# Row scales applied where outputs are drained, a new opening order, and packed queries in a two-block transformer kernel

## The reference

```python
mem_n = rmsnorm(mem, mem_norm_g)                      # 256 memory tokens
hn = rmsnorm(x, attn_norm_g[0])
proj = hn @ w_in                                      # c_q 384 | c_kv 256 | k_r 32 | q_cross 256
q = (rmsnorm(c_q, q_norm_g) @ w_uq).reshape(b, s, 12, 96)
q = concat([q[..., :64], rope(q[..., 64:], positions)])
kv = (rmsnorm(c_kv, kv_norm_g) @ w_ukv).reshape(b, s, 12, 64 + 64)
k = concat([kv[..., :64], broadcast(rope(k_r, positions))])
o = causal_dense_attention(q, k, kv[..., 64:])
cross = memory_cross_attention(q_cross, mem_n, w_mem_kv[i])
x = x + concat([o, cross]) @ w_o[i];  x = x + squared_relu_mlp(rmsnorm(x), ...)
```

## Time and profile before

| | |
|---|---|
| three timed runs | 1968.14, 1969.76, 1969.70 us (median 1969.7) |
| profiled execution | 1970.45 us, span 1968.5 us |
| busy in the span: TensorE, VectorE, ScalarE, GpSimd | 98%, 46%, 39%, 48% |
| chain that ended last | TensorE 90%, VectorE 5%, issue 3%, ScalarE 2% |
| mean granted TensorE clock | 0.989 of 2.4 GHz |

### The profile page before, as it was taken

How to read it: one execution, slowest core, us unless ns; L and a number is a source line. 1 busy time by engine, 2 the same in 40 slices (tenths; PEclk the granted TensorE clock), 3 DMA queues, 4 the chain that set the end, 5 groups by cost and what they waited for, 6 DMA issues and landing times.

```text
span 1968.5 us, 27142 instructions
## 1 busy us (share of the span) xinstructions
PE 1932.1 (98%) x9314; PEld 1590.0 (81%) x9314; DVE 897.3 (46%) x1840; ACT 770.5 (39%) x1375; POOL 944.3 (48%) x1236
## 2 busy tenths in 40 slices
PE   7999999999999999999999999999999999999999
PEld 6867878888888888788888876678988888888887
DVE  7877732222226585422223474676722345444200
ACT  4537743223233476432232452326832342232221
POOL 5750155555546542555555564432045546555653
PEclk9999999999999999999999999979999999999999
DMA  5330023232222301232323232111023223233332
GB/s 216 100 110 1 12 97 97 96 97 96 96 96 91 101 29 33 91 98 95 101 93 99 93 117 77 53 54 44 1 84 98 95 78 107 96 96 98 105 107 75
DMA packets 47086, 168.46 MB, mean 86 GB/s; under 512 B 5328, under 2 KB 5648, under 8 KB 46736
## 3 DMA queue, kind: packets, MB, share of 16 engines
q1 hardware_dynamic: 45792, 164.54, 25.7%
q10 hardware_dynamic: 1200, 2.64, 0.5%
HBM read 164.28 MB, written 2.10 MB: 85 GB/s over the span
## 4 chain that ended last, share of the span: by engine, by line
PE 90%; DVE 5%; issue 3%; ACT 2%; POOL 0%; DVEq 0%; POOLq 0%; ACTq 0%
PE bank L559 26%; PE bank L560 26%; PE bank L561 26%; PE bank L664 4%; PE bank L637 3%; PE bank L650 2%; DVE XL L1271 1%; ACT PROB L948 1%; PE bank L821 1%; PE bank L731 0%; PE bank L604 0%; POOL WL L520 0%; DVE KT L1284 0%; PE bank L616 0%; PE bank L661 0%
## 5 line engine op out<-in xcount | busy, mean ns | idle before, releaser
L520 POOL TENSOR_TENSOR WL<-RAW,WH 128x256 fp32r<-128x256 f32 x1208 | 927.0, 799 | 980.3 <-ACT WH L884 980.1
L559 PE MATMUL bank<-XH,WH 128*128 128x512 f32 (+2 forms) x1472 | 586.3, 398 | 5.7 <-DVE XL L1271 4.4
L560 PE MATMUL bank<-XL,WH 128*128 128x512 f32 (+2 forms) x1472 | 576.2, 391 | 0.0
L561 PE MATMUL bank<-XH,WL 128*128 128x512 f32 (+2 forms) x1472 | 575.8, 391 | 0.0
L884 ACT ACTIVATE WH<-RAW 128x1024 fp32r<-128x1024 f32 x302 | 317.2, 1052 | 360.0 <-PE bank L561 359.4
L559 PEld LDWEIGHTS bank<-XH,WH 128*128 128x128 f32 (+2 forms) x1472 | 276.5, 188 | 79.5 <-issue 10.4
L560 PEld LDWEIGHTS bank<-XL,WH 128*128 128x128 f32 (+2 forms) x1472 | 276.6, 188 | 61.7 <-issue 4.1
L561 PEld LDWEIGHTS bank<-XH,WL 128*128 128x128 f32 (+2 forms) x1472 | 276.6, 188 | 60.3
L559 PE MATMUL bank<-HH,WH 128*128 128x512 f32 x512 | 199.2, 389 | 0.0
L561 PE MATMUL bank<-HH,WL 128*128 128x512 f32 x512 | 199.2, 389 | 0.0
L560 PE MATMUL bank<-HL,WH 128*128 128x512 f32 x512 | 199.2, 389 | 0.0
(11 more groups left out here) (346 smaller groups left out, 2611.5 us busy)
## 6 DMA issues: line engine op xcount, KB each, us to landing
RAW<-stream SPq DMA_DIRECT2D x302, 512.0 KB, 3.6
X<-x SPq DMA_DIRECT2D x4, 512.0 KB, 7.0
out<-X SPq DMA_DIRECT2D x8, 256.0 KB, 4.6
MEM<-mem SPq DMA_DIRECT2D x1, 1024.0 KB, 10.9
W<-cmp_w ACTq DMA_DIRECT2D x1, 1024.0 KB, 4.8
KT<-KR ACTq DMA_DIRECT2D x1, 768.0 KB, 6.2
CT<-consts SPq DMA_DIRECT2D x1, 656.0 KB, 12.6
POSB<-pos_rows ACTq DMA_DIRECT2D x2, 256.0 KB, 2.6
```

What stands on the lines that cost most here:

```text
L520: ins = pool.tensor_tensor(WL[:, slot, c], RAW[:, slot, c], WH[:, slot, c].bitcast(F32), ALU.subtract)
L559: pe.matmul(dst, lhs[0], rhs[0], start=start, stop=False)
L560: pe.matmul(dst, lhs[0], rhs[1], start=False, stop=False)
L561: return pe.matmul(dst, lhs[1], rhs[0], start=False, stop=stop)
```

## The change

Six things change, all before the first attention.

1. **Opening.** SyncE loads the first eight gain columns, x 0, x 1, weight tile 0 and the rest of x in five pieces; the early constants and other gains move from ScalarE's queue to SyncE's, behind weight tile 1. VectorE sets ACC to ones, ScalarE reads one column of it, and TensorE multiplies it three times in fp32 into bank 7. ScalarE rounds tile 0 after two x tiles instead of one.
2. **Three outputs by passes.** Outputs 0 to 2 of in0 first go through the WH passes, then the WL passes. The small products move: sums(in0) after output 1 as before but inside this scheme, scales(in0) after 3, sums(mem) after 4, scales(mem) after 5, sums(c_kv) after 6, scales(c_q) after mem output 5 instead of 6.
3. **mem.** Its operand is mem times gain, rounded straight from MEM, with its remainder made by one VectorE pass early; the row scale (RBM) and column scale (RMEM) are applied when outputs are drained.
4. **c_kv and c_q.** The c outputs are drained by ScalarE without a scale; the operand is C32 times gain in one VectorE pass; the inner norm's scale comes out of sums over the unscaled c (`of_normed`, with the x scale) and is applied at the drains of keys (RBC), values (RKV, by ScalarE) and queries (ACC).
5. **Queries.** The weight columns are regrouped: three outputs of 128 rows hold the rope parts of four heads each, six outputs hold the plain parts of two heads each. The three rope outputs are scaled, rotated and added on 128 rows, and ScalarE places 32 rows per head; the six plain outputs are drained like the keys.
6. **Attention's entry** waits for all but two drains, and for the other two at its second and third unit.

```diff
-    up += [(3 + h // 3, (h % 3 * KQ + k) * QK, QK, k, 14 + h) for h in range(NH) for k in range(KQ)]
-    p.stage("up0", 7, 26, up)
+    up += shift(by_output(NROPE + NH // 2, KQ), 3, FIRST_Q)      # NROPE = 3, FIRST_Q = 14
+    p.stage("up0", 7, FIRST_Q + NROPE + NH // 2, up)
...
@ sync
-            for j in range(RING):
-                sp.dma_start(X[:, 2 * j:2 * j + 2, :], x[:, 2 * j:2 * j + 2, :]).then_inc(x_in[j], 16)
-                if j == 0:
+            sp.dma_start(GV[:, 0:KD], gains[:, 0:KD]).then_inc(signal("first_gains_in"), 16)
+            for first, n in X_PIECES:          # ((0, 1), (1, 1), (2, 2), (4, 2), (6, 2))
+                sp.dma_start(X[:, first:first + n, :], x[:, first:first + n, :]).then_inc(x_in[first], 16)
+                if first == 1:
                     load(0, 0, stream[0])
             load(1, 1, stream[1])
+            sp.dma_start(CT[:, 0:CONST_LATE], consts[:, 0:CONST_LATE]).then_inc(consts_in, 16)
+            sp.dma_start(GV[:, KD:], gains[:, KD:]).then_inc(consts_in, 16)
             load(2, 2, stream[2])
...
@ tensor
+            def warm_up():
+                pe.wait_ge(signal("acc_set"), 1)
+                for _ in range(3):
+                    ins = pe.matmul(BANK[7][:], ACC[:, 0:P], ACC[:], start=True, stop=True)
+                ins.then_inc(signal("acc_read"), 1)
+
+            def first_outputs(n, after):
+                steps = [plan.steps["in0"][j * KD:(j + 1) * KD] for j in range(n)]
+                for j in range(n):
+                    pe.wait_ge(hi_done, j + 1)
+                    for a, part in ((XH, "in0_x_hi"), (XL, "in0_x_lo")):
+                        for t, c, width, k, o, _, _, _ in steps[j]:
+                            if j == 0:
+                                pe.wait_ge(signal(part), k + 1)
+                            pe.matmul(BANK[o % RING][:], WH[:, t % RING, c:c + width], a[:, k, :],
+                                      start=k == 0 and part == "in0_x_hi", stop=False)
+                for j in range(n):
+                    pe.wait_ge(lo_done, j + 1)
...                                                # the WL products of output j, then after[j]
+            first_outputs(3, {1: sums("in0")})
+            dense(lambda _: plan.steps["in0"][3 * KD:], 0, operand(XH, XL), o0=plan.out0["in0"],
+                  after={3: [scales("in0", diagonal=TMP[:, 0, :])], 4: [sums("mem", NMEM)], 5: [scales("mem", NMEM)],
+                         6: [sums("c_kv")]})
...
+                pe.wait_ge(drained, plan.out0["up0"] + FIRST_Q + r + 1)      # rotate_query(r), r < 3
+                pe.matmul(BANK[6 + r % 2][:], const("rot_mla", 0, P), TMP[:, r % 2, :], start=True, stop=True)
...
@ scalar, in order
+            for m in range(KD): ... x_hi("in0", "attn0", m); after m == 1: keep_ahead(in0, 0)
+            keep_ahead(in0, 1); squares of x, with keep_ahead(in0, 2) after the fourth; keep_ahead(in0)
+            for m in range(KD):
+                act.activation(MH_[:, m, :], MEM[:, m, :], ACT.Copy, scale=gain("mem", m)).then_inc(signal("mem_hi"), 1)
+            std("in0"); keep_ahead(in0 + 2); c_out(0..2); keep_ahead(in0 + 3); squares of mem
+            c_out(3); keep_ahead(in0 + 4); c_out(4); std("mem", NMEM); keep_ahead(in0 + 5)
+            c_square("c_kv", 0, 0); keep_ahead(in0 + 6); c_square("c_kv", 0, 1); std("c_kv")
+            keep_ahead(in0 + 7); keep_ahead(memo); act.wait_ge(products_done, plan.out_mark[in0 + 7])
+            for j in range(KKV + KQ):
+                act.activation(XH[:, j, :], C32[:, j, :], ACT.Copy, scale=norm_gain).then_inc(signal("c_hi"), 1)
...
+                for i in range(4):                 # for each rope output r
+                    ins = act.activation(QT0[HD:QK, 4 * r + i, :], TMP[ROPE * i:ROPE * (i + 1), r % 2, :], ACT.Copy)
+                ins.then_inc(signal("q0_placed"), 1)
...
@ vector, in order
+            remainders of x; acc_read; add_square("in0", 0..7); remainders of mem (one pass each)
             scale_columns("in0", D, diagonal=TMP[:, 0, :])
             for m in range(KD):
                 add_square("mem", m, NMEM)
             scale_rows("in0", RBC)
-            c_out(0..2); scale_columns("mem", D, NMEM)
             angles0(0)
-            c_out(3); scale_rows("mem", ACC, NMEM); mem in two passes a tile, c_out(4) inside
+            scale_columns("mem", D, NMEM, dst=RMEM)
             angles0(1)
+            scale_rows("mem", RBM, NMEM)
             add_square("c_kv", 0..1); KR; memory queries
+            for j in range(KKV + KQ):
+                dve.scalar_tensor_tensor(XL[:, j, :], C32[:, j, :], norm_gain, XH[:, j, :].bitcast(F32),
+                                         ALU.mult, ALU.subtract).then_inc(signal("c_lo"), 1)
...
+            for m in range(6):
+                both_halves(up0 + m, KT0[0:HD, :, :], m, RBC)
+            def query_rope(r):
+                if r >= 2:
+                    dve.wait_ge(signal("q0_placed"), r - 1)
+                dve.tensor_tensor(TMP[:, r % 2, :], output(up0 + FIRST_Q + r)[:], ACC[:], ALU.mult).then_inc(drained, 1)
...
+            query_rope(0); query_rope(1); query_turned(0); query_rope(2); query_turned(1)
+            for m in range(NH // 2):
+                both_halves(up0 + FIRST_Q + NROPE + m, QT0[0:HD, :, :], m, ACC)
+                if m == 0:
+                    query_turned(2)
```

More of the change, by code:

```diff
@@ L707, in _ @@
-            pe.wait_ge(consts_in, 32)
-            first_output(plan.steps["in0"][:KD])
-            dense(lambda _: plan.steps["in0"][KD:], 0, operand(XH, XL), o0=plan.out0["in0"],
-                  after={1: [sums("in0")], 2: [scales("in0", diagonal=TMP[:, 0, :])], 3: [sums("mem", NMEM)], 4: [scales("mem", NMEM)],
-                         7: [sums("c_kv")]})
+            def warm_up():
[3 more added lines that the diff above has]
+                ins.then_inc(signal("acc_read"), 1)
@@ L1032, in _, with c_out, c_square @@
+            def c_out(j):
+                act.wait_ge(products_done, plan.out_mark[in0 + j])
+                act.activation(C32[:, j, :], BANK[(in0 + j) % RING][:], ACT.Copy).then_inc(drained, 1)
+            def c_square(norm, first, j):
+                act.wait_ge(drained, in0 + first + j + 1)
+                square(norm, j, C32[:, first + j, :])
             std("in0")
-            keep_ahead(in0 + 1)
-            act.wait_ge(mem_in, 16)
+            keep_ahead(in0 + 2)
+            for j in range(3):
+                c_out(j)
@@ L1047, in c_squares @@
-            def c_squares(norm, first):
-                for j in range(NORM_K[norm]):
-                    square(norm, j, C32[:, first + j, :])
-            def c_hi(first, n):
-                for j in range(first, first + n):
-                    act.wait_ge(signal("c_scaled"), j + 1)
-                    act.activation(XH[:, j, :], TMP[:, j % 2, :], ACT.Copy).then_inc(signal("c_hi"), 1)
-            act.wait_ge(drained, in0 + 2)
-            c_squares("c_kv", 0)
+            keep_ahead(in0 + 5)
@@ L1067, in _ @@
+            for j in range(KQ):
+                c_square("c_q", KKV, j)
+                if j == 0:
+                    keep_ahead(memo + 1)
+            for j in range(2):
+                split_q((drained, in0 + 7 + j), PROB1[:, j, :], QX[:, 2 * j:2 * j + 2, :])
             keep_ahead(memo + 3)
             std("c_q")
+            act.wait_ge(signal("angles0"), 2)
             act.activation(COS0[:], COS0[:], ACT.Sin).then_inc(signal("sines0"), 1)
@@ L1071, in _ @@
             keep_ahead(memo + 4)
-            for j in range(2):
-                split_q((drained, in0 + 7 + j), PROB1[:, j, :], QX[:, 2 * j:2 * j + 2, :])
-            keep_ahead(memo + 5)
             for j in range(2):
@@ L1443, in _ @@
             scale_rows("in0", RBC)
-            def c_out(j):
-                dve.tensor_tensor(C32[:, j, :], output(in0 + j)[:], RBC[:], ALU.mult).then_inc(drained, 1)
-            def angles0(part):
-                angles(POSB0[:], POSF0[:], const("inv_mla"), ANG0[:, 0, :], ANG0[:, 1, :], COS0[:], SIN0[:], "angles0",
-                       parts=(part,))
-            for j in range(3):
-                c_out(j)
-            scale_columns("mem", D, NMEM)
             dve.wait_ge(signal("pos_in"), 32)
```

265 lines of the change are left out of this document (122 added, 143 removed).

## The result

The changed kernel takes 1952.6 us (median of four runs, 1949.9 to 1954.0) where the kernel before takes 1969.7: ratio 0.9912, 95% interval 0.9895 to 0.9929, or 17.2 us less. 1950.0 was predicted, with 1943.5 to 1958.5 as the range. The time falls in it, but for partly wrong reasons: the 4.5 us forecast ahead of the query stage did not appear there, and 3.2 us came behind it, where the prediction saw nothing. The profiled execution took 1954.0 us around a span of 1952.1.

A forecast was written before the change was run, and what follows sets the result against it. It took TensorE, busy almost throughout, as the bound. Query stage 15.2 plus 4.5 ahead of it made 19.7 us, nothing afterwards: 1970.45 to 1950.7, then 1950.0 because neighbour runs' median stood 0.7 lower; range 1943.5 to 1958.5.

The forecast's parts named there:

- Query stage, 15.2: From the first query product to attention's first reduction: 23.0 us instead of 38.2, so 15.2 us less.
- The 0.2275 us a product: TensorE's full-pace time per product, used for the 81 query products: 18.4 us.
- Front, 4.5: Everything ahead of the query stage: key drains, and so the query stage, start 3 to 5 us earlier, taken as 4.5.
- The prediction's own sign of being wrong: Among the signs listed as showing the prediction wrong: a query stage that starts after 112.
- in0's end: Output 7 of in0 ends and mem starts at 61.8 us, where mem started at 66.0 before.
- The terms listed for the key drains: From 61.8, tile, roundings, squares, splits, diagonal, rotations and copies put the first key drain at 92.7 or 94.7, before 97.64.
- at the old rates they are in at 5.4: Opening: the first 1.0 MB, through weight tile 0, arrives by 5.4 us at 174, then 417 GB/s.
- unless they start after 2.0: Opening: three fp32 products of ones, at most 1.7 us each, cost nothing unless started after 2.0 us.
- The waits were forecast at 3.1 and 1.8: In in0, TensorE waits 3.1 us for the mem diagonal after output 5 and 1.8 us after output 6.
- the fourth rival: In in0, the 3.1 us wait closes the clock, costing 1.6 us, or 3.2 if twice: 1953.2 us; chance 0.10.
- Afterwards, 0: Everything after the query stage is the same instructions, so no time changes there: 0 us.
- the second rival: Ahead of the query stage nothing is gained, VectorE's chain from in0 to keys staying as long: 1954.5 us; chance 0.22.

The follow-up runs named there:

- queries alone: Kernel before with only the packed query outputs and attention's new entry (parts 5 and 6), c_q still scaled at the operand: 1957.2 us, second time 1957.5.
- tile 0 first: On the changed kernel with angles behind the diagonals and memory splits behind key drains (1946.6 us): weight tile 0 loaded and rounded before x; 1945.6 us.
- one by passes: Changed kernel with only output 0 of in0 made by passes, outputs 1 and 2 going k by k as before: 1951.5 us.
- attention's entry: Changed kernel with part 6 undone, attention's first scores waiting for all drains: 1952.8 us.

## Why the prediction was right, and where it was wrong

**Query stage, 15.2: right in size, half right in cause.** 23.0 was forecast and 23.3 measured. The rotations stand where the list put them, the third with the forecast wait of 0.4 us. A placing copy took 0.63 us (0.6 assumed between nothing and 0.72), a scaled drain 0.69. But the sum assumed that VectorE is ready when the stage begins. The queries alone show that this is the work of the moved scales (2.7 us); the term was counted in the right total and under the wrong edit. The 0.2275 us a product doesn't follow from the 41.05 and 2.6 given for it (they give 0.229); the spacing in the traces is 0.227, so nothing hangs on it.

**Front, 4.5: wrong, -1.6.** The prediction's own sign of being wrong, a query stage that starts after 112, came true, and the first reduction stands at 137.8 where 131 was named. The step that failed is in0's end, predicted at 61.8 and measured at 67.8. From there the list of VectorE held: last in0 product to first key drain 31.65 us, where 30.9 to 32.9 was forecast, and 14.93 us more to the query stage (15.16 before). (The terms listed for the key drains add up to 92.0 and 93.7, not 92.7 and 94.7; the copy of a row scale, 0.68 us, isn't among them.) The 6.0 us have three parts:
- *First product, 2.4 late* (9.46 for 7.1). The bytes were costed at the rates of the earlier trace rows, which belong to another order of transfers: 174 and 417 GB/s became 133 and 355, and tile 0 could be rounded at 8.35 instead of 6.1. The step "at the old rates they are in at 5.4" carried this. By itself it wouldn't have mattered: with tile 0 first, the start is at 6.9 and the remainders of x begin no earlier than in the earliest of the other traces.
- *First product to third output, 2.0 longer* (21.75 for 19.7). The ones were costed at nothing "unless they start after 2.0". They started at 1.5 and still cost 0.5 to 0.8 us through the clock, by the run without them. The rest is x: output 0's high products and remainders were forecast to end at 13.3, and ended at 17.5 (16.3 in the second trace), and that is nearly all of this part and the one above.
- *Third output to in0's end, 1.6 longer* (36.6 for 35.0). The waits were forecast at 3.1 and 1.8 and came as 0.75 and 2.61, 1.5 less in all; but 58.1 to 65.0 went at the lower clock level, 3.4 us lost. This is the fourth rival, which had the right mechanism with the wrong wait: the fall came with the second, and 1.6 was given as its price, 3.2 if it fell twice. The 1.6 was read short too: in the kernel before, the lower level lasts to 70.05, not 3.4 us but 4.0 from mem's first product on, and costs 2.0.

In the kernel before, the first eight products go with x, 0.6 us apart; from 14.0 to 15.2 they come 0.43 us apart, as they do at the lower level at 285, and from 15.6 on 0.23 apart: TensorE starts at the lower level. The Trainium skill (TensorE: Matmul & The Clock Gate, Part 1: The HAM clock gate) says the same of a cold start, and that the moment of the rise differs from run to run. The trace agrees: the first record of the upper level is at 15.4 and at 14.5 in the two traces of the queries alone. So read, the page speaks for products of ones, but no run here shows a gain by them, with three or with six.

**Afterwards, 0: wrong, -3.2.** "Everything after it is the same instructions" holds, and the time differs all the same. Two falls of the clock of before are absent. By stretch, the kernel before, the changed kernel, and the queries alone:

```profile
152.00:155.40 3.40, 3.40 (x10) 1.87 (x9) 3.25 (x16) 2.81 (x11) 0.00 (x0) 0.50 0.00 0
285.00:288.40 3.40, 3.40 (x10) 2.62 (x10) 2.81 (x7) 2.36 (x3) 3.13 (x5) 0.51 0.09 10
```

```profile
139.00:142.40 3.40, 3.13 (x13) 1.69 (x12) 3.38 (x17) 2.61 (x10) 0.77 (x2) 1.00 0.68 233
271.00:274.40 3.40, 3.40 (x16) 2.77 (x17) 2.78 (x7) 2.29 (x3) 3.15 (x5) 1.00 0.01 1
```

```profile
142.00:145.40 3.40, 3.16 (x17) 1.94 (x16) 3.38 (x17) 2.83 (x10) 0.31 (x1) 1.00 0.61 208
274.00:277.40 3.40, 3.40 (x10) 2.66 (x9) 2.28 (x7) 1.81 (x3) 3.14 (x5) 0.51 0.20 25
```

At attention's entry TensorE waited 1.6 us before and 0.8 now, and attention is 0.8 us shorter (81.88 to 81.04). At 285 it had waited 1.2 us for VectorE; the same 1.2 us stands in the changed kernel, without the fall, and that stage goes from 92.78 to 91.15. The fall at 285 is there in the trace of before and in both of the queries alone, and in none of the eleven traces that hold the front edits. The two stages make 2.5 of the 3.2 us; the other 0.7 lies behind them, where the falls of the clock differ from trace to trace. Why the same wait is followed by a fall in the one family and not in the other was not settled: no kernel here changed only the distance from the front.

**The sum.** -15.2 - 4.5 + 0 was forecast, -14.8 + 1.6 - 3.2 = -16.4 measured on the spans: an error of 6.1, one of 0.4 and, with the opposite sign, one of 3.2. That the time lies within 3 us of the forecast is in part luck. So is that the front edits are worth 5.7 us beside the forecast 4.5: what they give lies in the query stage and behind it, not ahead of it. The time also lies 2 us from what the second rival gives (1954.5: the front brings nothing), and ahead of the query stage it is that one by mechanism, with the fourth beside it.

## What to carry to other kernels

Cost a stage together with what its feeder is still doing when it begins: 2.7 us of this gain belong to edits made in earlier stages, which without the packed queries gained nothing. When a wait is shortened, put independent work (here sine angles) behind the small product that TensorE needs next; moving it gave 4.5 us without removing an instruction. A change of a few microseconds ahead of a long tail also moves falls of the clock in the tail, so count the tail's stages in both traces before the sum is called right.

## What the runs showed of the hardware

- Products of ones ahead of the work raised the clock early and it fell again: up at 6.9 us, down at 10.35, after 2.5 us of idle time, for 6.8 us. With six of them and the idle time at 0.3 us it didn't fall. The clock column shows 1.00 ahead of the first record (0 to 5 us above), while the records of ones come 0.85 us apart there and 0.43 apart from 6.4 on, when there are six of them: the lower level; in that stretch the spacing tells, not the column.
- A wait of 2.6 us in in0 went with 6.8 us at the lower level in five traces and with 3.4 in two (one by passes, attention's entry); the same wait of 3.5 us in the front of before with 6.8 in two and 3.4 in one; and one of 1.2 us was followed by 3.4 in three traces and by nothing in eleven.
- The first 10 us of transfers don't follow the rate of another order: with the gain columns and single x tiles in front, 133 GB/s over the first 5 us (114 in the second trace) instead of 174; with the old order in the changed kernel it was 171. Two profiled runs of one kernel had tile 0 usable 1.1 us apart (first products at 9.46 and 8.36).
